# An encoder trunk with an expert layer on one core: stage orders rewritten, experts' results scattered in two single-pass halves

## What is computed

```python
def rms_norm(x, g):
    y = xf * lax.rsqrt(jnp.mean(xf * xf, axis=-1, keepdims=True) + NORM_EPS)
    return (y * g).astype(x.dtype)

def moe_swiglu(h, router, wg, wu, wd):
    top_v, top_i = lax.top_k((h @ router).astype(jnp.float32), TOP_K)
    comb = jnp.sum(one_hot(top_i, N_EXPERTS) * softmax(top_v)[..., None], axis=-2)
    for e in range(N_EXPERTS):
        out = out + comb[..., e:e + 1] * swiglu(h, wg[e], wu[e], wd[e])

for l in range(DEPTH):
    hn = rms_norm(h, attn_norm[l]);  p = hn @ w_in[l]
    ...                                    # the three mixers, gated and summed: merged
    h = h + merged @ w_o[l]
    hn = rms_norm(h, ffn_norm[l])
    h = h + (swiglu(hn, ...) if l % 2 == 0 else moe_swiglu(hn, ...))
return rms_norm(h, final_norm)
```

## Time and profile before

| | us |
|---|---|
| median of 3 runs | 2103.09 (2100.44 to 2105.04) |
| the profiled execution | 2101.6 |
| its span, first to last instruction | 2099.7 |
| PE busy in the span | 1975.3 (94%) |
| DVE busy | 1375.4 (66%) |
| ACT busy | 1110.4 (53%) |
| mean granted TensorE clock, share of full | 0.978 |

### The profile page before, as it was taken

The page is one execution under the profiler, slowest core; times in us unless marked ns, Lnnn a source line. Parts: engine busy times, 40 slices in busy tenths (PEclk is TensorE's granted clock), DMA queues, the critical chain, the costliest instruction groups (busy, mean ns, idle before and its releaser), DMA issues.

```text
span 2099.7 us, 23988 instructions
## 1 busy us (share of the span) xinstructions
PE 1975.3 (94%) x9114; PEld 1514.9 (72%) x9114; DVE 1375.4 (66%) x1377; ACT 1110.4 (53%) x1089; POOL 103.9 (5%) x124
## 2 busy tenths in 40 slices
PE   6999999899989999999789999999999999999997
PEld 5865666478878756665478787887878878787886
DVE  4672444344445654344288888888888888888886
ACT  4565111234344554111177677776767777677764
POOL 1350000000000520000000000000000000000000
PEclk9999998999999999998899999999999999999999
DMA  9532031544546422031199898998989989898993
GB/s 327 176 121 103 18 121 60 206 143 161 194 151 213 145 86 80 1 144 58 59 340 354 318 370 321 352 357 325 371 321 353 356 326 365 326 350 323 354 364 140
DMA packets 181490, 485.66 MB, mean 231 GB/s; under 512 B 5880, under 2 KB 12660, under 8 KB 172600
## 3 DMA queue, kind: packets, MB, share of 16 engines
q1 hardware_dynamic: 176256, 475.53, 62.0%
q0 software_dynamic: 1488, 5.57, 0.7%
q10 hardware_dynamic: 3688, 3.74, 0.7%
HBM read 480.06 MB, written 1.05 MB: 229 GB/s over the span
## 4 chain that ended last, share of the span: by engine, by line
PE 85%; DVE 6%; ACT 4%; issue 2%; POOL 1%; DMA 1%; ACTq 0%; DVEq 0%; SPq 0%
PE bank L1438 40%; PE bank L1014 17%; PE bank L1006 7%; PE bank L1114 6%; PE bank L1408 1%; PE bank L1392 1%; PE bank L1469 1%; DVE w_lo L1499 1%; ACT w_hi L942 1%; PE bank L1220 1%; DMA ring<-moe_w_gate_dram 1%; DVE xg_lo L1926 1%; PE bank L1233 1%; DVE xterm L1499 1%; PE bank L1190 1%
## 5 line engine op out<-in xcount | busy, mean ns | idle before, releaser
L1499 DVE TENSOR_TENSOR w_lo<-ring,w_hi 128x2048 fp32r<-128x2048 f32 x336 | 764.0, 2289 | 154.6 <-ACT w_hi L942 154.6
L942 ACT ACTIVATE w_hi<-ring 128x2048 fp32r<-128x2048 f32 x336 | 643.3, 1916 | 160.4 <-PE bank L1438 159.4
L1438 PE MATMUL bank<-w_hi,xg_hi 128*128 128x512 f32 x896 | 354.4, 395 | 9.0 <-DVE w_lo L1499 9.0
L1438 PE MATMUL bank<-w_hi,xg_lo 128*128 128x512 f32 x896 | 350.5, 391 | 0.0
L1438 PE MATMUL bank<-w_lo,xg_hi 128*128 128x512 f32 x896 | 350.4, 391 | 0.0
L1438 PEld LDWEIGHTS bank<-w_hi,xg_hi 128*128 128x128 f32 x896 | 169.5, 189 | 44.9 <-DVE w_lo L1499 10.8
L1438 PEld LDWEIGHTS bank<-w_hi,xg_lo 128*128 128x128 f32 x896 | 168.7, 188 | 35.7
L1438 PEld LDWEIGHTS bank<-w_lo,xg_hi 128*128 128x128 f32 x896 | 169.0, 189 | 33.9
L1438 PE MATMUL bank<-w_hi,ehT_hi 128*128 128x512 f32 x448 | 177.5, 396 | 3.5 <-DVE w_lo L1499 3.5
L1438 PE MATMUL bank<-w_lo,ehT_hi 128*128 128x512 f32 x448 | 175.1, 391 | 0.0
L1438 PE MATMUL bank<-w_hi,ehT_lo 128*128 128x512 f32 x448 | 175.0, 391 | 0.0
(11 more groups left out here) (383 smaller groups left out, 2690.3 us busy)
## 6 DMA issues: line engine op xcount, KB each, us to landing
ring<-moe_w_gate_dram SPq DMA_DIRECT2D x56, 2048.0 KB, 7.9
ring<-moe_w_up_dram SPq DMA_DIRECT2D x56, 2048.0 KB, 8.5
ring<-moe_w_down_dram SPq DMA_DIRECT2D x56, 2048.0 KB, 8.3
ring<-w_in_dram SPq DMA_DIRECT2D x26, 2048.0 KB, 8.6
ring<-w_branch_dram SPq DMA_DIRECT2D x6, 2048.0 KB, 11.6
ring<-ffn_w_gate_dram SPq DMA_DIRECT2D x5, 2048.0 KB, 8.1
ring<-ffn_w_up_dram SPq DMA_DIRECT2D x5, 2048.0 KB, 8.2
ring<-ffn_w_down_dram SPq DMA_DIRECT2D x5, 2048.0 KB, 7.6
```

What stands on the lines that cost most here:

```text
L942: A.activation(w_hi[:, q % PARTS, :], ring[:, i, o:o + HALF], ACT.Copy).then_inc(s.hi_ready, 1)
L1438: ins = M(dst, a, w, start=start and n == 0, stop=stop and n == 2, skip_group_check=True)
L1499: return V.tensor_tensor(out_, a, b, op)
```

## The change

1. **Norms by token tile.** `norm_sums`, `normalise` and the transposes work on one token tile at a time (`transpose_rows`, jobs `nT{t}{u}`, `fT{t}{u}`). DVE applies the gain straight from PSUM (`transposed`), ACT and DVE make the halves of the activations by quarter (`ix_hi`, `ix_low`, `fx_low`). The output projection runs o00, o10, o01, then the transposes of tile 0, then o11. The dense feed-forward starts with tile 0 and has the transposes of tile 1 behind the first 12 matmuls; the router does tile 0 first.
2. **Halves in dense stages.** Four buffers for hi instead of two, lo is written in place into the ring (`ring_lo`), and a slot is free when PE is through with the panel instead of when lo is written.
3. **Last transposes later.** `turn(6)` in the expert stage and `turn(5)` in the dense one stand behind the first down panel.
4. **Scatter.** `selT` is the 0/1 selection in fp32r, ACT writes `ey_hi` after hi(1), DVE `ey_lo`, PE does eight single-pass matmuls instead of four of float32. DVE applies the combine weight (`weight`) where it adds to h, by scalar_tensor_tensor.
5. **Orders.** `xg_lo` stands ahead of lo(36) instead of behind it. The first raise of `lo_ready` stands ahead of the output projection's additions in layer 1. The router's weights are loaded at the program's start. Two dummy Sqrt activations put the table switch ahead of the norms.

```diff
@@ layer_jobs @@
-    out = [(f"nT{q}", A) for q in range(4)]
+    out = [(f"nT{t}{u}", V) for u in range(2) for t in range(T)]
-    out += [(f"o{u}{t}", V) for u in range(2) for t in range(T)]
-    out += [(f"fT{q}", A if l else V) for q in range(4)]
+    out += [(n, V) for n in ("o00", "o10", "o01", "fT00", "fT01", "o11", "fT10", "fT11")]
@@ build @@
-    i_hi = sb("i_hi", [P, 2, HALF], F32R, where=B + 16384)
-    i_lo = sb("i_lo", [P, 2, HALF], F32R, where=B + 32768)
+    i_hi = sb("i_hi", [P, 4, HALF], F32R, where=B + 16384)
-    ey = sb("ey", [P, D], where=X + 97280)
+    ey_hi = sb("ey_hi", [P, D], F32R, where=X + 97280)
+    ey_lo = sb("ey_lo", [P, D], F32R, where=X + 108544)
-        if kind.startswith("ffn"):
-            return s.f_lo_ready, 2 * (n - FIRST_FFN + 1)
-        if kind == "in":
-            return s.i_lo_ready, 2 * (9 * l + j + 1)
+        if kind == "ffn_down" and j < 5:
+            return s.f_half_used, 12 + 2 * (j + 1)
...
@@ gpsimd, at its start @@
+        pool.dma_start(router[:], moe_router[0].rearrange("(c p) n -> p c n", p=P)).then_inc(s.router_loaded, 16)
@@ scalar @@
+        def norm_sums(m, t):
+
+            own.step(A.activation(hn[:, t, :], h[:, t, :], ACT.Square, accum_out=stat[:, 0, t:t + 1]), s.sumsq_ready)
+            act.wait_ge(s.var_ready, T * m + t + 1)
+            own.step(A.activation(stat[:, 0, t:t + 1], stat[:, 0, t:t + 1], ACT.Sqrt), s.root_ready)
...
             for q in range(2 * EP):
                 hi(q)
+                if q == 1:
+                    down_hi(lambda job: item_product(job, len(ITEM)))
...
+        down_hi(last_product)
+        A.activation(den[:, 0, 0:1], C("ident", 0, 1), ACT.Sqrt)
         act.wait_ge(s.items_done, 1)
-        norm_sums(4)
+        for t in range(T):
+            norm_sums(4, t)
@@ tensor, scatter @@
-                    done(M(b_of(f"sc{u}{t}")[:], cselT[:, t * P:(t + 1) * P], ey[:, 512 * u:512 * u + 512],
-                           start=True, stop=True))
+                    b = b_of(f"sc{u}{t}")
+                    for i, part in enumerate((ey_hi, ey_lo)):
+                        ins = M(b[:], selT[:, t * P:(t + 1) * P], part[:, 512 * u:512 * u + 512], start=i == 0,
+                                stop=i == 1)
+                    done(ins)
@@ tensor, expert loop @@
             for j in range(7):
+                if j == 1:
+                    turn(6)
                 item_read_out(f"eT{j}")
@@ vector @@
+            if l == DEPTH - 1:
+                V.tensor_copy(smax[:, 1, :], smax[:, 0, :]).then_inc(s.lo_ready, 2 * RING)
...
+                dve.wait_ge(s.ey_hi_ready, n + (u + 1))
+                tt(ey_lo[:, cols], b[:], ey_hi[:, cols].bitcast(F32), ALU.subtract).then_inc(s.freed_vec, 1)
...
-                    ins = tt(hs, bank_of(f"sc{u}{t}")[:], hs, ALU.add).then_inc(s.freed_vec, 1)
+                    V.scalar_tensor_tensor(out=hs, in0=bank_of(f"sc{u}{t}")[:], scalar=weight[:, 1, t:t + 1], in1=hs,
+                                           op0=ALU.mult, op1=ALU.add).then_inc(s.freed_vec, 1)
...
-                if q == 36:
-                    gathered_lo(item_product, item * 9 + 9)
...
+                if q == 35:
+                    gathered_lo(item_product, item * 9 + 9)
```

More of the change, by code:

```diff
@@ L176, in layer_jobs @@
                 out += [(f"hT{j - 1}{t}", V) for t in range(T)]
-        out += [(f"fd{u}{t}", V) for u in range(2) for t in range(T)]
+        out += [(f"fd{u}{t}", V) for t in range(T) for u in range(2)]
     else:
@@ L882, in _ @@
                 ffn_high(1)
-            read_out(act, f"o11.{l}")
-            norm_sums(2 * l + 1)
-            if l:
-                norm_transposed("fT", l, 1)
-            else:
-                for q in range(4):
-                    b = product(act, f"fT{q}.0")
-                    for i in range(2):
-                        c = 2 * q + i
-                        own.step(A.activation(fx_hi[:, c, :], b[:, 256 * i:256 * i + 256], ACT.Copy,
-                                              scale=gains[:, 0, 1, c:c + 1]), s.f_x_hi_ready if i else None)
+            for t in range(T):
+                read_out(act, f"o1{t}.{l}")
+                norm_sums(2 * l + 1, t)
+                for u in range(2 if l == 0 else 0):
+                    four, tok = slice(4 * u, 4 * u + 4), slice(t * P, (t + 1) * P)
+                    read_out(act, f"fT{t}{u}.0")
+                    own.step(A.activation(fx_hi[:, four, tok], fxT[:, four, tok], ACT.Copy), s.f_x_hi_ready)
+            if l == 0:
                 for q in range(2, 36):
@@ L903, in _ @@
                             own.free(A.activation(sg[:, j % 2, t, 0:w_], b[:, 0:w_], ACT.Silu), f"fg{j}{t}.0")
+                        if j == 5:
+                            own.step(A.activation(den[:, 0, 0:1], C("ident", 0, 1), ACT.Sqrt))
                     if q % 4 == 1 and 9 <= q <= 29:
@@ L922, in gathered_hi, with down_hi @@
                 ins.then_inc(s.x_hi_ready, 1)
+        def down_hi(eng_wait):
+            for u in range(2):
+                A.activation(ey_hi[:, 512 * u:512 * u + 512], eng_wait(f"ed{u}")[:], ACT.Copy)\
+                    .then_inc(s.ey_hi_ready, 1)
         gathered_hi(lambda job: ahead(act, job))
@@ L988, in done, with transpose_rows, transpose_in @@
             ins.then_inc(s.product_ready, 1)
-        def transpose_in(jobs, src, blocks=False):
+        def transpose_rows(job, src, t, u, blocks=False):
+            b = bank(job)
+            for i in range(4):
+                n = 4 * u + i
+                cols = slice(n * P, n * P + P) if blocks else slice(n, D, KD)
+                ins = TR(b[:, i * P:(i + 1) * P], src[:, t, cols], ident)
+            done(ins)
+        def transpose_in(jobs, src):
             for q in range(4):
@@ L1351, in _ @@
+                outs = [(u, t, bank(f"fd{u}{t}.0")) for t in range(T) for u in range(2)]
                 for j in range(6):
+                    used[0] += 1
+                    if j == 1:
+                        turn(5)
                     read_out(pe, f"hT{j}1.0")
@@ new lines, in turn @@
+            def turn(j):
+                item_read_out(f"eu{j}")
+                b = item_bank(f"eT{j}")
+                for c in range(4):
+                    ins = TR(b[:, c * P:(c + 1) * P], ehm[:, j % 2, c:512:4], ident)
+                done(ins)
+            item_read_out_before("gx1")
+            for j in range(7):
+                for g, name in enumerate(("eg", "eu")):
+                    b = item_bank(f"{name}{j}")
+                    for r in range(2):
+                        q = 4 * j + 2 * g + r
+                        half(q)
+                        for c in range(4):
+                            x = 4 * r + c
+                            ins = three(b[:], xg_hi[:, x, :], xg_lo[:, x, :], q % PARTS,
+                                        slice(512 * c, 512 * c + 512), x == 0, x == KD - 1)
+                        if r == 0:
+                            ins.then_inc(s.half_used, 1)
+                    done(ins)
+                    if j == g == 0:
+                        scatter(item, item_bank)
+                        b = item_bank("csT")
+                        for t in range(T):
+                            ins = TR(b[:, t * P:(t + 1) * P], sel[:, t, :], ident)
+                        done(ins)
+                if j:
+                    turn(j - 1)
@@ L1533, in _ @@
         for l in range(DEPTH):
-            normalise(2 * l, hn)
+            if l == 0:
+                dve.wait_ge(s.gain_loaded, 16 * 4 * DEPTH)
+            for t in range(T):
+                normalise(2 * l, t, hn)
             def in_lo(q):
```

326 lines of the change are left out of this document (168 added, 158 removed).

## The result

The changed kernel takes 2045.32 us (median of 4 runs, 2044.75 to 2046.48), the kernel before 2103.01 beside it: ratio 0.9727, with a 95% interval of 0.9710 to 0.9744. The prediction was 2042.5 in a range of 2032 to 2064. Its profiled execution has a span of 2042.9 us, where that of before had 2099.7: 56.8 us less.

What follows compares the result with a forecast made beforehand. PE was taken to bound the kernel, with DVE and DMA within a seventh in an expert pass. Gains of 32.0 + 9.0 + 5.3 + 1.5 + 2.7 + 8.5 + 1.4 = 60.4 us gave 2042.5 us, range 2032 to 2064.

Steps and rivals of the forecast that it cites:

- The scatter: Expert pass: eight single-pass matmuls replace four float32 ones, gaining 1.61 us in each pass, all on PE.
- The last turn in the expert stage: Expert pass, ahead of the down panels: last four transposes move behind 24 down matmuls, gaining 2.1 us a pass.
- q = 37: Expert pass: with xg_lo in DVE's idle time lo(37) comes 1.5 us sooner, PE's wait goes; gain 0.6 us a pass.
- What these edits add in a pass: Start of an expert pass: added ACT and DVE work, tight ahead of lo(4), charged 0.3 us a pass, bounds 0 and 2.5.
- Output projection to feed-forward: Layer 0, between these stages: shorter norm wait, partly covered by 12 matmuls; gain 9.7 us worked out, 9.0 taken.
- Last transposes of the dense part: End of the dense feed-forward: PE's 3.70 us wait for the last hm goes, with one half-clock stretch; gain 5.3 us.
- Buffers and ring in the dense stages: Input projections and dense stages: gain 1.5 us at the start, 2.7 at layer 1's start; later slot freeing costs nothing.
- Router and first expert: Layer 1, router to first expert panel: 5.5 us from router and norm, 3.0 from earlier weight loads; gain 8.5 us.
- Final norm: End of the program: no table switch and the first tile's output leaves earlier; gain 1.4 us.
- Loads: Rival: the loads set the expert pass, which stays at 128 us; total 2074.5 us; chance one in ten.
- DVE at the pass's start: Rival: DVE late there, 2.2 us more each expert pass, 2060 us; 14 in a hundred, including transposes only moving their wait.
- a load a lap late: Rival: an expert pass's first load comes late, kernel slower than before, 2115 us at 18 us landing; three in a hundred.

Runs made afterwards that it cites:

- the one with both edits: Changed kernel with ring, hnT and hn 32 bytes further on, and hm of the last dense round behind lo(24): 2034.14 us, ratio 0.9661 to the kernel before.

## Why the prediction was right, and where it was off

**The scatter**: right. 1.61 worked out, 1.62 measured by undoing it.

**The last turn in the expert stage**: right, 2.1 forecast, 1.95 measured. What it missed is that such a wait can bring half clock behind it; 1.6 us in the last pass of before, which I had only in the low end. That low end was too low even so: its own terms lead to some 2037, and one stretch of 1.6 us, all that the trace before shows, to 2035 and not to 2032.

**q = 37**: 0.6 forecast, 0.8 measured.

**What these edits add in a pass**: 0.3 us charged, nothing measured; the term failed. The three gains without it are 1.62 + 1.95 + 0.8 = 4.37, and a pass is 4.34 shorter in the middle six (127.97 to 123.62 on average). So the 4.4 us that the eight passes gave beyond the forecast are mostly these eight times 0.3 and the 1.6 of half clock. The place was named rightly. DVE there, timeline of the changed kernel:

```profile
1412.63 1.28 DVE L1550 TENSOR_TENSOR ey_lo<-bank,ey_hi 128x512 fp32r<-128x512 f32 x2
1413.83 4.48 DVE L1550 TENSOR_TENSOR w_lo<-ring,w_hi 128x2048 fp32r<-128x2048 f32 x2
1418.23 2.72 DVE L2024 SCALAR_TENSOR_TENSOR h<-bank,weight,h 128x512 f32<-128x512 f32 x4
1420.88 2.29 DVE L1550 TENSOR_TENSOR w_lo<-ring,w_hi 128x2048 fp32r<-128x2048 f32 x1
```

The 1.54 us of idle time ahead of lo(4) in the earlier trace rows is used up, but four scalar_tensor_tensor take 2.72 us, where the four additions in the same place took 2.48 (at 1450.34 in the trace before): 0.24 us more, and PE does not wait for it. Groups by line, this form after and the addition before:

```profile
L2024 DVE SCALAR_TENSOR_TENSOR h<-bank,weight,h 128x512 f32<-128x512 f32 x36 | 24.5, 744 | 0.0
```

```profile
L1499 DVE TENSOR_TENSOR h<-bank,h 128x512 f32<-128x512 f32 x48 | 30.8, 683 | 41.0 <-PE bank L1006 39.1 <-PE bank L1014 1.1 <-PE bank L1408 0.7
```

744 ns against 683; the upper bound of twice the time was far off, the row of the same operation at another size (342 ns for 128 columns) near.

**Output projection to feed-forward**: right, 9.0 forecast and 9.55 measured up to the end of the first four panels. The wait of 0.6 us behind 12 matmuls that I worked out is 0.59 in the trace, and without those 12 it is 3.61.

**Last transposes of the dense part**: wrong, 5.3 forecast; from the last up product to the first down product 1.7 gained (5.69 to 4.01 us), and over the rest of the stage, slower matmuls included, 0.9. The step that failed is "the wait of 3.70 us goes". I followed the data of `hm` to the transposes and moved with them, and did not ask what else waits for `hm`: the down products need four banks, and in the order of the jobs these are the banks of the last gate and up products, which DVE frees with the same `hm`. The wait stayed, at 2.76 us, under another name. Moving `hm` one step up on DVE took 2.20 of it. The half clock behind the wait is gone in the changed kernel's trace, but by luck: of the ten traces with this wait at 2.6 to 2.8 us seven have 3.4 us at half clock at the start of the down panels, and the stretch is then 1.6 us longer. The two with `hm` moved have none.

**Buffers and ring in the dense stages**: wrong, at both places. The buffers were costed at 1.2 us of gain in an input projection, and reading lo from the ring at nothing. The wait at the second input panel is 1.55 and 1.64 us where the earlier trace rows had 1.19: the first panel reaches PE sooner and DVE's chain of lo halves sets it. And reading lo out of the ring, at the address where it stood, cost 5.3 us in three stages. The layer 1 stretch shows it: the norm gave 4.64 us, and the input projection took 4.04 back, 2.20 of it by slower matmuls. The prediction had asked only whether in-place writes would be slow for DVE, never whether PE's reads would be.

**Router and first expert**: 8.5 forecast, 7.3 measured. Up to the routing 4.7 instead of 5.5, with a wait of PE of 1.69 us for the norm of tile 1 between the two halves of the router that I had not listed; the loads 2.55 instead of 3.0, of which only 1.0 lasts. I had written that half clock on the first matmuls would stay as it is; it grew by what came sooner. The sign that I gave, the first expert matmul some 27 us sooner, failed: it is 18.5 us sooner (1055.25 to 1036.74), since the dense part gave 3.9 us less than forecast, layer 1's start 2.1, this stage 1.2, and the mixers of both layers together ran 1.1 us longer.

**Final norm**: 1.4 forecast, 1.9 measured. The table load has moved ahead of the wait (ACT's timeline):

```profile
2029.80 1.28 ACT L965 ACT_TABLE_LOAD   x1
2031.10 0.20 ACT L965 ACTIVATE den<-cst 128x1 f32<-128x1 f32 x1
2033.38 1.06 ACT L676 ACTIVATE hn<-h 128x1024 f32<-128x1024 f32 x1 [2.08 <-DVE smax L2086]
```

The next activation again starts 1.30 us after the load's start.

**The rivals.** None came. Loads: PE is busy for the whole pass, and by then they reach 356 GB/s on average, so 344 was no limit. It is nearer than I had it, though: share 0.97. DVE at the pass's start has no idle time left, and PE none to wait. Nothing shows a load a lap late.

## What to carry to other kernels

Work out a moved step from the place where it stands, and follow every user of what the waiting instruction frees: a bank that is reused is as good a reason to wait as the data. Compare stretches between the same instructions and not only totals; here a total within 4 us of the forecast held a stage 4 us better and three that were 7 us worse. When buffers move or are shared, look at the matmuls' start-to-start time in the stages around it, before and after: 227 against 234 ns is invisible in any single wait and cost as much as two of the waits that were removed.

## What was not expected of the hardware

**Addresses set the pace of single-pass matmuls.** With 512 columns, start to start, in the input projections and the dense down panels: 227 ns where the operands all stand at 32 modulo 64 bytes, 229 where all stand at 0, 231 to 234 where some stand at 0 and some at 32. Changing only the ring's place by 32 bytes moved 336 matmuls from 78.63 to 76.43 us. These 336 take 76.42 or 76.43 us in all six traces with every operand of theirs at 32, but with lo read from the ring at 0 and the rest at 32 they take 78.62 or 78.63 us in five and 77.89 in two (the float32 scatter, and `hm` moved alone), at the same addresses; so a part of the price differs between executions for another reason. Also open: the gate and up panels take 232 to 233 ns wherever `fx_hi` stands at 0, with the ring at 0 or at 32 and even with all at 0, and the expert stage does not mind (123.47 against 123.60), so the place modulo 64 is not all of it. Which access of PE is slowed was not tried.

**Half clock moves whole stages without an edit.** The mixers of a layer are the same instructions in all these kernels, and the two layers' have as many. Their stretch, with the mean granted clock in the eighth column (the changed kernel in layer 1; then layer 1 of the kernel with `xg_lo` late; layer 0 of the one with both edits):

```profile
721.43:979.14 257.71, 239.69 (x1211) 153.80 (x1211) 118.06 (x257) 74.31 (x144) 14.04 (x26) 0.97 0.22 81
```

```profile
720.37:972.41 252.04, 234.06 (x1210) 149.63 (x1210) 117.95 (x257) 74.17 (x144) 14.02 (x26) 0.99 0.23 83
```

```profile
121.95:384.07 262.12, 244.20 (x1210) 157.19 (x1211) 118.05 (x256) 74.31 (x144) 16.66 (x31) 0.95 0.23 83
```

From 252 to 262 us, for the same work. DVE and ACT are busy for the same time in all; PE alone is slower, by stretches at half clock (1.2 instead of 2.4 GHz) that begin behind or between its waits in some executions and not in others. The spread of one kernel's runs, 1.4 to 10 us, goes with the clock: the kernel before took 2099.78 us at a mean granted clock of 0.979 and 2109.46 at 0.971. This is why the changed kernel's 2.66 us lost and 1.52 gained in the mixers say nothing on the change.
